# Reordering the first norm of each layer: squares behind the loads of x, rounding in turn with scale and shift

## The reference

```python
mod = silu(c) @ w_ada[layer] + b_ada[layer]          # 6 x 1024 per condition row
sh1, sc1, g1, sh2, sc2, g2 = split(mod, 6)
h = x * rsqrt(mean(x*x) + EPS) * norm1[layer] * (1 + sc1) + sh1
```

## Time and profile before

| | us |
|---|---|
| median of 3 runs | 1270.45 |
| profiled execution | 1268.03 |
| its span | 1266.2 |
| TensorE busy | 1136.2 (90%) |
| VectorE busy | 494.3 (39%) |
| ScalarE busy | 321.2 (25%) |
| GpSimd busy | 45.2 (4%) |
| mean granted TensorE clock | 0.939 of full |

### The profile page before, as it was taken

One profiled execution on the slowest core, in us unless ns is written; L12 is line 12 of the kernel. 1 busy time (PEld: TensorE's weight loads), 2 busy tenths in 40 slices (PEclk: granted clock), 3 DMA queues, 4 the chain that ended last, 5 costly groups with the idle time before them and its releaser, 6 DMA issues.

```text
span 1266.2 us, 17985 instructions
## 1 busy us (share of the span) xinstructions
PE 1136.2 (90%) x7492; PEld 761.9 (60%) x7492; DVE 494.3 (39%) x1222; ACT 321.2 (25%) x608; POOL 45.2 (4%) x94
## 2 busy tenths in 40 slices
PE   3869999879697999999997899978897999999996
PEld 2669777667365555555544799645465455555544
DVE  0257443433525233333334433454425233333334
ACT  0166301122003111111112443454313111111114
POOL 0010000300001000000000200200001000000000
PEclk9579999979798999999999899999997999999998
DMA  9644221479483599999996344698680899999951
GB/s 282 200 134 134 67 75 59 132 245 343 161 331 133 205 412 382 368 376 367 372 360 214 102 150 151 224 330 306 229 324 18 325 409 383 362 364 376 373 197 43
DMA packets 122884, 317.18 MB, mean 250 GB/s; under 512 B 9136, under 2 KB 93136, under 8 KB 96166
## 3 DMA queue, kind: packets, MB, share of 16 engines
q1 hardware_dynamic: 115652, 304.87, 65.5%
q0 software_dynamic: 2336, 7.84, 1.9%
q10 hardware_dynamic: 4802, 3.18, 1.1%
HBM read 309.37 MB, written 6.49 MB: 249 GB/s over the span
## 4 chain that ended last, share of the span: by engine, by line
PE 80%; DVE 11%; ACT 3%; issue 2%; DMA 1%; SPq 1%; ACTq 0%; DVEq 0%
PE bank L1556 17%; PE bank L1127 11%; PE bank L1577 9%; PE bank L1519 5%; PE bank L1594 4%; PE bank L1190 4%; PE bank L1224 3%; PE bank L1091 3%; PE bank L1092 3%; PE bank L1093 3%; PE bank L1182 2%; DVE arena L2019 2%; DVE xT L2025 2%; PE bank L1086 2%; PE bank L1537 1%
## 5 line engine op out<-in xcount | busy, mean ns | idle before, releaser
L1556 PE MATMUL bank<-arena 128*64 128x512 f32 x768 | 225.2, 593 | 0.5 <-DVE gslot L2468 0.5
L1556 PEld LDWEIGHTS bank<-arena 128*64 128x64 f32 x768 | 71.7, 137 | 108.7 <-issue 108.0
L1715 ACT ACTIVATE arena<-bank 128x512 f32<-128x512 f32 (+7 forms) x159 | 78.6, 525 | 209.0 <-PE bank L1093 53.0
L1577 PE MATMUL bank<-ring,scratch 128*64 128x512 f32 x512 | 116.9, 599 | 1.1 <-ACT scratch L1715 1.1
L1556 PE MATMUL bank<-ring,arena 128*64 128x512 f32 x256 | 112.5, 592 | 0.0
L1091 PE MATMUL bank<-hTh,wh 128*128 128x320 f32 x304 | 96.2, 316 | 14.0 <-DVE wl L2084 14.0
L1127 PE MATMUL bank<-hT,ring 128*128 128x320 f32 x352 | 98.0, 435 | 0.6 <-issue 0.6
L1092 PE MATMUL bank<-hTl,wh 128*128 128x320 f32 x304 | 95.6, 314 | 0.0
L1093 PE MATMUL bank<-hTh,wl 128*128 128x320 f32 x304 | 95.5, 314 | 0.0
L2025 DVE SCALAR_TENSOR_TENSOR xT<-bank,mod,xT 128x256 f32<-128x256 f32 x144 | 69.1, 480 | 66.3 <-PE bank L1127 55.7
L2025 DVE SCALAR_TENSOR_TENSOR scratch<-scratch,gslot,bank 128x256 f32<-128x256 f32 x32 | 21.7, 678 | 163.3 <-ACT scratch L1935 163.3
(11 more groups left out here) (312 smaller groups left out, 1696.4 us busy)
## 6 DMA issues: line engine op xcount, KB each, us to landing
ring<-in_w_exp_down_dram SPq DMA_DIRECT2D x64, 1024.0 KB, 9.2
arena<-in_w_exp_gate_dram SPq DMA_DIRECT2D x48, 1024.0 KB, 8.8
arena<-in_w_exp_up_dram SPq DMA_DIRECT2D x48, 1024.0 KB, 11.3
ring<-in_w_ada_dram SPq DMA_DIRECT2D x44, 1024.0 KB, 9.7
ring<-in_w_exp_gate_dram SPq DMA_DIRECT2D x16, 1024.0 KB, 11.1
ring<-in_w_exp_up_dram SPq DMA_DIRECT2D x16, 1024.0 KB, 10.4
ring<-in_w_in_even_dram SPq DMA_DIRECT2D x14, 1024.0 KB, 5.4
ring<-in_w_qkv_odd_dram SPq DMA_DIRECT2D x8, 1024.0 KB, 5.4
```

The source lines that it names most:

```text
L1556: ins = pe.matmul(bank[0][SLOTS * w:SLOTS * w + SLOTS, :].rearrange("p (w f) -> p w f", w=2), hg[:, q % 2, c, s0:s0 + SLOTS], weights[w][: ...
L1577: ins = pe.matmul(bank[2 + d][rows, :], hidT[:, P * f + SLOTS * w:P * f + SLOTS * w + SLOTS], x[:, w, D * f + 512 * d:D * f + 512 * d + 51 ...
L1715: return act.activation(dst, src, ACT.Copy)
```

## The change

1. In the head of layer 0 the squares become a ScalarE step of their own (`squares`), in its queue ahead of row 4's copy, so that each follows its chunk of x. VectorE adds the squares of the chunks together (`accumulate`, with tag "01"), one addition between the copies of x, and TensorE sums one chunk instead of eight.
2. The root stays behind turn 2; the spreading (`nbc`) and the multiplication `xn` move behind row 6 and turn 4.
3. In both layers the ScalarE order after the gain becomes: four chunks of `hp`, then `hh` of a chunk and `hp` of the chunk four further on in turn. The first three half units of weights move: in layer 0 two ahead of the gain on ScalarE and directly behind it on VectorE, in layer 1 one ahead of `hp` and one in the middle; the third comes behind the last `hh` (and `hl`).
4. GpSimd's samples: in layer 0's first norm the multiplication by the root goes to `tiny` and doesn't wait for the gain; in the other three norms the multiplication by the gain comes first and doesn't wait for the root.
5. TensorE no longer waits for the last `hp` and the samples ahead of the projection.

```diff
@@ plan_head
                         makes("head", "dve", ("x", c))
+                        if c >= 2:
+                            makes("head", "dve", ("acc", "01", c - 1))
+                    makes("head", "dve", ("acc", "01", C - 1))
+                    makes("head", "act", ("squares",))
                 if u == 4:
                     fills("head", ("stats",), ("act", "std01"))
                     makes("head", "act", ("stats",))
                     makes("head", "dve", ("root",))
+                if u == 6:
                     fills("head", ("nbc",), ("dve", ("xn01", C - 1)))
                     makes("head", "dve", ("stats",))
...
@@ gpsimd: norm_samples
-                after(pool, "dve", f"gain{tag}")
-                after(pool, "dve", f"rs{tag}")
...
-                link(pool.tensor_tensor(hs, xs, of_token, ALU.mult))
-                link(pool.tensor_tensor(hs, hs, gainA[:, :, 1:NCOND].unsqueeze(3).to_broadcast([P, C, NB, LS]), ALU.mult))
+                of_row = gainA[:, :, 1:NCOND].unsqueeze(3).to_broadcast([P, C, NB, LS])
+                if tag == "01":
+                    after(pool, "dve", f"rs{tag}")
+                    part = tiny[:, :].rearrange("p (c b t) -> p c b t", c=C, b=NB)
+                    link(pool.tensor_tensor(part, xs, of_token, ALU.mult))
+                    after(pool, "dve", f"gain{tag}")
+                    link(pool.tensor_tensor(hs, part, of_row, ALU.mult))
+                else:
+                    after(pool, "dve", f"gain{tag}")
+                    link(pool.tensor_tensor(hs, xs, of_row, ALU.mult))
+                    after(pool, "dve", f"rs{tag}")
+                    link(pool.tensor_tensor(hs, hs, of_token, ALU.mult))
...
@@ tensor: norm, head
-                after(pe, "act", (f"hp{tag}", C - 1))
-                after(pe, "pool", f"hs{tag}")
...
                     elif what == "stats":
-                        for c in range(C):
-                            norm_sum("01", c)
+                        after(pe, "dve", ("acc", "01", C - 1))
+                        claim(pe, k)
+                        filled(token_squares(B(k), C - 1, True, True), k)
...
@@ scalar: norm_apply
+                if j == 3:
+                    for c in range(C):
+                        shifted(c)
+                    return
+                split_half(l, 0)
+                if l == 0:
+                    split_half(l, 1)
+                    after(act, "dve", "gain01")
+                for c in range(4):
+                    shifted(c)
+                after(act, "pool", f"hs{tag}")
+                for c in range(C):
+                    rounded(c)
+                    if c + 4 < C:
+                        shifted(c + 4)
+                    if l == 1 and c == 2:
+                        split_half(l, 1)
+                split_half(l, 2)
...
@@ vector: norm_stats, norm_apply
                     result("dve", (f"xn{tag}", c), mul(scratch[:, c, 0:NP_], xT[:, c, 0:NP_], B(k)[:, 0:NP_]))
+                    if tag == "11" and c == 3:
+                        split_half(1, 0)
...
                     l = int(tag[0])
+                    if l == 0:
+                        split_half(0, 0)
+                        split_half(0, 1)
                     for c in range(C):
...
+                        if l == 1 and c == 2:
+                            split_half(1, 1)
+                    split_half(l, 2)
```

More of the change, by code:

```diff
@@ L706, in normed @@
         def normed(tag):
-            return [(f"xn{tag}", 0), f"rs{tag}"] + [(f"xn{tag}", c) for c in range(1, C)]
+            return [(f"xn{tag}", 0), f"rs{tag}"] + [(f"xn{tag}", c) for c in range(1, 4)] + \
+                ([("lo", 1, 0)] if tag == "11" else []) + [(f"xn{tag}", c) for c in range(4, C)]
         DVE_ORDER = []
@@ L713, in trunk_program @@
         for l in range(2):
-            DVE_ORDER += ["gain11", "root11"] + normed("11") if l else ["gain01"]
-            DVE_ORDER += [("hl", l, c) for c in range(C)]
+            DVE_ORDER += ["gain11", "root11"] + normed("11") if l else ["gain01", ("lo", 0, 0), ("lo", 0, 1)]
+            for c in range(C):
+                DVE_ORDER += [("hl", l, c)] + ([("lo", 1, 1)] if l == 1 and c == 2 else [])
+            DVE_ORDER += [("lo", l, 2)]
             if l == 0:
@@ L718, in trunk_program @@
             else:
-                DVE_ORDER += [("lo", 1, n) for n in range(24)] + [("vt", i) for i in range(6)]
+                DVE_ORDER += [("lo", 1, n) for n in range(NH, 24)] + [("vt", i) for i in range(6)]
                 DVE_ORDER += steps_of("mixer1", "dve")
             for m in range(C):
-                DVE_ORDER += [(f"xo{l}", m)] + ([("acc", l, m - 1)] if m >= 2 else [])
-            DVE_ORDER += [("acc", l, C - 1), f"gain{l}2", f"root{l}2"] + normed(f"{l}2")
+                DVE_ORDER += [(f"xo{l}", m)] + ([("acc", f"{l}2", m - 1)] if m >= 2 else [])
+            DVE_ORDER += [("acc", f"{l}2", C - 1), f"gain{l}2", f"root{l}2"] + normed(f"{l}2")
             DVE_ORDER += [f"rt{l}", f"rm{l}", f"oh{l}", f"rt2{l}", f"chosen{l}"] + [(f"hk{l}", i) for i in range(4)] + [f"rank{l}"]
@@ L726, in trunk_program, with first_chunks @@
         DVE_ORDER += ["rootf"] + [("yt", i) for i in (1, 3, 5)]
+        def first_chunks(l):
+            order = [("hi", l, 0)] + ([("hi", l, 1)] if l == 0 else []) + [(f"hp{l}1", c) for c in range(4)]
+            for c in range(C):
+                order += [("hh", l, c)] + ([(f"hp{l}1", c + 4)] if c + 4 < C else []) + \
+                         ([("hi", l, 1)] if l == 1 and c == 2 else [])
+            return order + [("hi", l, 2)]
         ACT_ORDER = []
         for step in steps_of("head", "act"):
-            ACT_ORDER += [("sq01", c) for c in range(C)] + ["std01"] if step == ("stats",) else [step]
+            ACT_ORDER += [("sq01", c) for c in range(C)] if step == ("squares",) else ["std01"] if step == ("stats",) else [step]
         for l in range(2):
-            ACT_ORDER += (["std11"] if l else []) + [("hp%d1" % l, c) for c in range(C)] + [("hh", l, c) for c in range(C)]
+            ACT_ORDER += (["std11"] if l else []) + first_chunks(l)
             if l == 0:
@@ L1734, in norm_apply, with shifted @@
             def norm_apply(tag):
-                if tag == "01":
-                    after(act, "dve", "gain01")
                 if tag == "02":
                     after(act, "pool", "mixer0")
-                j = 0 if tag[1] == "1" else 3
-                for c in range(C):
+                l, j = int(tag[0]), 0 if tag[1] == "1" else 3
+                def shifted(c):
                     after(act, "dve", (f"xn{tag}", c))
@@ L1744, in norm_apply, with rounded @@
                         hT[:, c, 0:NP_], scratch[:, c, 0:NP_], ACT.Identity,
[L1745 to L1748, removed]
-                    for c in range(C):
-                        after(act, "act", (f"hp{tag}", c))
-                        result("act", ("hh", l, c), copy(hTh[:, c, :], hT[:, c, :]))
+                        scale=gainA[:, c, 0:1], bias=mod[:, l, j, c, 0:1]))
+                def rounded(c):
+                    after(act, "act", (f"hp{tag}", c))
+                    result("act", ("hh", l, c), copy(hTh[:, c, :], hT[:, c, :]))
+                if j == 3:
+                    for c in range(C):
+                        shifted(c)
[7 more added lines that the diff above has]
+                after(act, "pool", f"hs{tag}")
+                for c in range(C):
+                    rounded(c)
[4 more added lines that the diff above has]
+                split_half(l, 2)
             def split_half(l, n):
@@ L1980, in _ @@
                     result("act", ("cond",), act.activation(condT[:, :, 0:NCOND], cols[:, :, 17:26], ACT.Silu))
+                elif what == "squares":
+                    act.wait_ge(ld_const, 16)
+                    norm_squares("01")
                 elif what == "stats":
-                    norm_stats("01")
+                    norm_std("01")
                 else:
@@ L2034, in mid, with accumulate @@
                 return ap.unsqueeze(2).to_broadcast([s[0], s[1], n, s[2]])
-            def accumulate(l, c):
-                after(dve, "act", (f"sq{l}2", c))
+            def accumulate(tag, c):
+                after(dve, "act", (f"sq{tag}", c))
                 if c >= 2:
-                    after(dve, "dve", ("acc", l, c - 1))
-                result("dve", ("acc", l, c), add(scratch[:, c, :], scratch[:, c, :], scratch[:, c - 1, :]))
+                    after(dve, "dve", ("acc", tag, c - 1))
+                result("dve", ("acc", tag, c), add(scratch[:, c, :], scratch[:, c, :], scratch[:, c - 1, :]))
             def norm_root(tag):
@@ L2305, in mixer1 @@
             def mixer1():
-                for n in range(24):
+                for n in range(NH, 24):
                     split_half(1, n)
@@ L2538, in _ @@
                     continue
+                if what == "acc":
+                    accumulate(*i)
+                    continue
```

27 lines of the change are left out of this document (8 added, 19 removed).

## The result

The changed kernel takes **1247.49 us** (median of 4 runs, 1245.94 to 1251.28) against 1270.12 (4 runs) for the kernel before beside it: a ratio of 0.9847, 95% interval 0.9808 to 0.9885. With two later batches (6 runs, median 1250.06; one run, 1250.51) its 11 runs have a median of 1248.98 us. The forecast was 1253.

The account below looks back on a forecast made before the run. The chain was taken to lie on TensorE almost everywhere, except two stretches the change touches. Head 14.5 plus layer 1 1.7 gave 1268.0 - 16.2 = 1251.8, plus half of 2.4 for the median: 1253 us, range 1246 to 1262.

Parts of the forecast that it names:

- The bound and the order of steps: Chain mostly on TensorE; in the head, sum right behind turn 2, then row 6 without waiting, first tile fed by chunks.
- Turn 2 to gain: Head of layer 0: shorter sum and new order make the gain ready at 55.8 instead of 66.53, 10.7 us earlier.
- Gain to second tile: Layer 0: rounding in turn with products brings the second projection tile sooner after the gain, 3.8 us.
- The conflict that I priced at 2.3 us: Layer 0 behind the gain: GpSimd's operations and VectorE's `lo` 0 and 1 take turns, delaying rounding to 60.5.
- Layer 1: Layer 1's first projection tile ready at 712.0 against 713.7, 1.7 us earlier, or 2.8 without the VectorE and GpSimd conflict.
- the filler matmuls keep the clock up: Layer 1: fillers until 706.80 bound the projection's start in either case and hold TensorE's clock up; no separate size.
- (a): No conflict between VectorE and GpSimd in either layer: 2.3 + 1.1 us more gain, 1249.6 us; chance 0.27.
- (b): Head's gain given back in a later stretch set by transfers, only layer 1's remaining: 1267.5 us; chance 0.12.
- (c): Chunk-fed first tile keeps TensorE at half clock, 2.9 us per further tile: 1256 to 1285 us; chance 0.06.
- (d): Row 6's weights late or rounding waits elsewhere, so only the shorter sum and layer 1 count: 1258.8 us; chance 0.09.
- The sum: Whole kernel: 14.5 us from the head plus 1.7 from layer 1, 16.2 together, giving 1251.8 for the profiled execution.

Follow-up runs that it names:

- e1: Changed kernel, but TensorE sums all eight chunks of squares again, without VectorE's additions; squares still early: 1258.81 us, ratio to the kernel before 0.9909.
- e2: Changed kernel with one-chunk sum, but squares and VectorE's additions moved back behind row 4's copy: 1257.05 us, ratio to the kernel before 0.9891.
- e9: The kernel before the change, unaltered, run again for the clock of its head: 1270.67 us, one run.
- e5: Changed kernel with layer 0's `hi` and `lo` 0 and 1 moved ahead of the gain: 1245.42 us, ratio to the kernel before 0.9827.
- e8: The changed kernel itself, unaltered, run again: 1250.06 us, ratio to the kernel before 0.985.
- e11: The changed kernel itself, unaltered, profiled a third time: 1250.51 us, one run.
- e6: Changed kernel with layer 1's `hi` 0 and 1 ahead of `hp`, `lo` 0 and 1 right behind the root: 1245.13 us, ratio to before 0.9834.
- e10: The kernel before the change, unaltered, run once more: 1274.53 us, one run.
- e3: Changed kernel keeping parts 1 and 2, with parts 3 to 5 undone in both layers: 1256.1 us, ratio to the kernel before 0.9904.
- e7: Changed kernel with the moves of e5 and e6 together: 1243.63 us, ratio to the kernel before 0.9814.

## Why the prediction was right, and where its sizes were off

**The bound and the order of steps: right.** Sum behind turn 2, row 6 behind it without a wait, rounding in turn with the products, the first tile fed chunk by chunk: every row stands where the forecast put it.

**Turn 2 to gain: right at half clock, 4.5 us too long at full clock.** The forecast put the end of the gain 13.7 us behind turn 2's start (55.8 less 42.14). At half clock it is 13.34 (13.11 and the gain's own 0.23), in both profiles of that kind; the sum was to take 1.25 and takes 1.29. The term that was mis-sized is TensorE's time in this stretch: I took every duration from rows at half clock. With the pause and the long sum gone, a clock that has risen lasts through the stretch, and in the first profile it had: 9.13 us (8.90 and 0.23) at 2.4 GHz. In e1 and e2, one profile each, either of the two things removed was enough to lose it.

**Turn 2's own start** lies between 40.47 and 42.07 us in the six profiles: the transposes of x take 7.66 to 9.20 us, by when the clock falls in them, in the kernel before too (7.79 in e9). Of the first profile's 21.1 us, 1.3 are this chance.

**Gain to second tile: right.** From the end of the gain 15.0 us were forecast and 14.31 measured, before 18.78. The conflict that I priced at 2.3 us costs 1.83 (4.48 less 2.65 from the gain to the first `hh`, change against e5). By the Trainium skill, SBUF — State Buffer, section Who interferes with whom, such a pair contends, and the lock is exclusive; the trace agrees that both suffer (GpSimd 2.05 and 1.94 instead of 1.08; the two `lo` 3.25 instead of 2.36 in e5). The rows that I leaned on showed less than I read in them: of the two copies in the earlier trace rows beside the same instruction, the first took 0.23 us and was not held up. That the conflict is there is shown by e5.

**Layer 1: 1.7 us forecast, 0.58 in the first profile, 1.8 and 1.4 in the other two, against the first profile of the kernel before.** The old order is itself no fixed mark: it took 16.55, 17.00 and 19.24 us. The forecast had `hi` 1 and `lo` 1 between chunks 2 and 3, and its last `hl` 7.0 us behind the first `hh`; the three profiles have 6.9. Where the clock stays up this gives the 1.7 (e8). What the forecast left out is the clock: `hl` 3 waits for both, so TensorE waits 1.88 us in the middle of its first tile (1.87 or 1.88 in the change, e5 and e8, 1.75 in e11), and in some profiles the clock falls behind that wait, at once (change: 0.50 over 2.8 us) or 1.5 us later (e5), in others not (e8, e11). e6 takes the wait away: 13.10. I also took it that the filler matmuls keep the clock up: it is 1.00 from 710 to 714 in the first two profiles of the kernel before, but 0.50 in e10, the one with 19.24.

**The rivals.** (a), no conflict, named 1249.6 us, within a microsecond of the median of all 11 runs, and is refuted all the same: the conflict is in the rows, and the clock gave what its absence was to give. (b), given back, didn't happen: between the second tile and layer 1, and from there to the end, the changed kernel's three profiles take no longer than the old one's (607 to 612 us against 611 to 612; 554 to 556 against 552 to 557). (c) falls with the clock of 0.99 from 58.6 on, through the second tile (24 x (0.27 - 3.52 / 24) is 2.96 us for a tile, not 2.9, which would have changed nothing); (d) falls with row 6 behind the sum without a wait.

**The sum.** Forecast for an execution like the profiled one: 1251.8 us. The two profiled executions at half clock took 1251.13 and 1250.51, the one at full clock 1245.94. That the first two come so near is in part luck: in e8, against the first profile of the kernel before, turn 2 starts 1.6 us earlier by chance, and the stretches outside the change together take 2.1 longer. The stretches that the change touches give 11.1, 4.5 and 1.8 us where 10.7, 3.8 and 1.7 were forecast.

**Open:** why the clock rises at 38 to 42 us in some executions and not in others. It did in seven of the nine profiles with the new head or a part of it (the change, e1, e2, e3, e5, e6, e7) and in none of the four with the old one. TensorE's work up to there is the same in both, as far as I can see; whether the change makes the rise likelier or chance does isn't settled.

## What to carry to other kernels

Price a step that closes a gap on TensorE at both clock levels: durations read beside the gap are those of the low one, and the work behind it may get faster too. Before moving an elementwise operation, look at what the other of VectorE and GpSimd does at that moment, and put the pair into a wait that both have anyway. When rounding is fed in turn with its consumer, keep pieces of another kind (here half a unit of weights) out of the middle of the queue: what stands behind them waits for them (1.88 us here), and the clock may fall behind the wait. And one profile is one draw of the clock: take a second before explaining its surplus.

## What the runs showed of the hardware

- During 48 matmuls of one column the granted clock fell while TensorE was busy without a break: 1.00 from 41 to 43.5, 0.51 from 43.5 to 49 (e1, one profile).
- One kernel, one order: the stretch from turn 2 to the gain took 8.90 us in one execution and 13.11 in two, at a granted clock of 1.00 from 42 to 46.7 us in the one and 0.50 in the two.
- Beside two VectorE subtractions with both inputs in SBUF, GpSimd's operations on 128x512 took 1.94 to 2.11 us instead of 1.08, and the subtractions 3.22 to 3.25 instead of 2.36; the multiplication beside `xn`, which reads PSUM, took 1.27, as beside nothing (1.26 in e3).
